# Attention scores of a gated recurrence: the matmuls and copies of each head cut to the blocks that the masks keep, in pieces of 32 queries

## What is computed

```python
G = jnp.cumsum(gc, axis=-2)                       # log decays, summed within a chunk of 64
diff = G[:, :, :, None, :] - G[:, :, None, :, :]
decay = jnp.exp(jnp.where(mask, diff, -jnp.inf))  # mask: key s <= query t
att = jnp.einsum('bhtk,bhsk,bhtsk->bhts', qc, kc, decay)
o = o_inter + jnp.einsum('bhts,bhsv->bhtv', att, vc)
```

## Time and profile before

| | |
|---|---|
| median of 3 executions | 2349.55 us (2348.75 to 2355.37) |
| profiled execution, first to last instruction | 2347.9 us |
| PE busy | 2281.0 us, 97% |
| DVE busy | 1565.2 us, 67% |
| ACT busy | 1268.0 us, 54% |
| POOL busy | 1337.0 us, 57% |
| score matmuls (L1168), 816 records | 30.3 us busy |
| large score copies (L2671), 48 | 35.1 us busy |
| small score copies (L2678), 24 | 5.3 us busy |

### The profile page before, as it was taken

How to read it: one execution, slowest core, us unless ns; L and a number is a source line. 1 busy time by engine, 2 the same in 40 slices (tenths; PEclk the granted TensorE clock), 3 DMA queues, 4 the chain that set the end, 5 groups by cost and what they waited for, 6 DMA issues and landing times.

```text
span 2347.9 us, 54490 instructions
## 1 busy us (share of the span) xinstructions
PE 2281.0 (97%) x20432; PEld 1959.8 (83%) x20432; DVE 1565.2 (67%) x2618; ACT 1268.0 (54%) x2295; POOL 1337.0 (57%) x1019
## 2 busy tenths in 40 slices
PE   8899999999998999999999999999999999999998
PEld 6788888888887888888878888877888888888886
DVE  7877777635589777777882332389687767445755
ACT  6454555433576666666554334554555544334775
POOL 2787777767515555555555444305777778677120
PEclk9999999999999999999999999999999999999999
DMA  3123222443530111111111212330232222535202
GB/s 132 50 83 101 92 77 86 151 143 103 166 100 20 40 46 46 44 39 41 49 43 49 63 48 86 115 101 28 86 92 89 86 77 86 178 122 194 76 19 75
DMA packets 155236, 194.93 MB, mean 83 GB/s; under 512 B 13168, under 2 KB 102512, under 8 KB 155120
## 3 DMA queue, kind: packets, MB, share of 16 engines
q1 hardware_dynamic: 111920, 153.59, 20.7%
q10 hardware_dynamic: 43200, 39.83, 5.2%
HBM read 155.49 MB, written 37.88 MB: 82 GB/s over the span
## 4 chain that ended last, share of the span: by engine, by line
PE 65%; DVE 13%; POOL 7%; issue 6%; ACT 5%; DMA 3%; SPq 1%; ACTq 0%; POOLq 0%; DVEq 0%
PE bank L1068 17%; PE bank L1071 17%; PE bank L1070 17%; PE bank L1035 4%; PE bank L1037 4%; PE bank L1036 4%; POOL ring L929 4%; DMA ring<-weights 3%; POOL ring L933 2%; DVE hid L2201 2%; DVE hid L2355 1%; DVE ops L2256 1%; DVE ops L2365 1%; DVE ops L2209 1%; PE bank L1201 1%
## 5 line engine op out<-in xcount | busy, mean ns | idle before, releaser
L1068 PE MATMUL bank<-ops,ring 128*128 128x264 f16 x4112 | 1139.4, 277 | 20.2 <-DVE work L2402 6.3
L1070 PE MATMUL bank<-ops,ring 128*128 128x264 f16 x4112 | 1138.7, 277 | 0.0
L1071 PE MATMUL bank<-ops,ring 128*128 128x264 f16 x4112 | 1138.6, 277 | 0.0
L929 POOL TENSOR_TENSOR ring<-ring 128x512 f16<-128x512 f32 (+1 forms) x492 | 659.8, 1360 | 273.8 <-ACT ring L1401 273.8
L1401 ACT ACTIVATE ring<-ring 128x512 f16<-128x512 f32 (+1 forms) x492 | 286.7, 614 | 501.8 <-POOL ring L933 498.3
L1068 PEld LDWEIGHTS bank<-ops,ring 128*128 128x128 f16 x4112 | 404.4, 98 | 91.3 <-issue 9.8
L1071 PEld LDWEIGHTS bank<-ops,ring 128*128 128x128 f16 x4112 | 403.7, 98 | 61.7
L1070 PEld LDWEIGHTS bank<-ops,ring 128*128 128x128 f16 x4112 | 403.7, 98 | 60.3
L914 POOL TENSOR_TENSOR ring<-wtmp,ring 128x512 f16<-128x512 f32 x107 | 130.8, 1227 | 340.9 <-ACT ring L1342 340.3
L1035 PE MATMUL bank<-hid,ring 128*128 128x264 f16 x1068 | 294.9, 276 | 1.5 <-issue 1.3
L1037 PE MATMUL bank<-hid,ring 128*128 128x264 f16 x1068 | 294.8, 276 | 0.0
(11 more groups left out here) (227 smaller groups left out, 3626.5 us busy)
## 6 DMA issues: line engine op xcount, KB each, us to landing
ring<-weights SPq DMA_DIRECT2D x363, 256.0 KB, 2.7
ops<-spill SPq DMA_DIRECT2D x16, 1056.0 KB, 6.9
ring<-weights SPq DMA_DIRECT2D x120, 128.0 KB, 2.4
spill<-hid ACTq DMA_DIRECT2D x42, 264.0 KB, 2.9
spill<-hid ACTq DMA_DIRECT2D x20, 528.0 KB, 5.0
ops<-spill SPq DMA_DIRECT2D x8, 792.0 KB, 5.1
hid<-xT SPq DMA_DIRECT2D x8, 528.0 KB, 8.3
hid<-out_x ACTq DMA_DIRECT2D x8, 528.0 KB, 7.3
```

The lines of the kernel that those rows point to most:

```text
L929: nc.gpsimd.tensor_tensor(low(slot, kh), weight_source(name, k, kh), high(slot, kh), ALU.subtract)\
L1068: nc.tensor.matmul(out, whi, xhi, start=(kk == 0 and fresh(name, k)), stop=False, skip_group_check=True)
L1070: nc.tensor.matmul(out, whi, xlo, start=False, stop=False, skip_group_check=True)
L1071: mm = nc.tensor.matmul(out, wlo, xhi, start=False, stop=end, skip_group_check=True)
```

## The change

`head_scores` computes only the pieces that a mask can keep, always 32 query columns wide, and all 17 chunks now lie 32 columns apart in the bank.
- L32: the chunk's keys 0 to 31 by its queries 32 to 63. 17 matmuls, each 32 x 32.
- L16: all 64 keys by the 32 queries that are in the last 16 of a block of 32 (two runs of 16 columns). 17 matmuls, each 64 x 32.
- D16: the two diagonal blocks of 32, as two matmuls of 32 x 32. 34 matmuls, whose results lie in partitions 0, 32, 64 and 96 onwards.

`evac_scores` follows. L32's kept part is a full rectangle, so it is a plain `tensor_copy`, 2 of 32 x 256 and 1 of 32 x 32. L16 takes 4 predicated copies of 64 x 128 and 2 of 64 x 16, D16 takes 4 of 32 x 256 and 2 of 32 x 32. The masks, the banks, the waits and the places in all queues are as before.

```diff
+            def score_parts(kind, kk, qq, c):
+                k0 = c * C
+                if kind == "L32":
+                    return [(0, kk[:, k0:k0 + 32], qq[:, k0 + 32:k0 + C])]
+                if kind == "L16":
+                    return [(0, kk[:, k0:k0 + C], qq[:, k0:k0 + C].rearrange("p (b t) -> p b t", b=2)[:, :, 16:32])]
+                return [(32 * n, kk[:, k0 + 32 * n:k0 + 32 * n + 32], qq[:, k0 + 32 * n:k0 + 32 * n + 32]) for n in range(2)]
...
-                            h0 = C * (c % 2)
-                            last = nc.tensor.matmul(bank[b][h0:h0 + C, (c - c0) // 2 * C:((c - c0) // 2 + 1) * C],
-                                                    kk[:, c * C:(c + 1) * C], qq[:, c * C:(c + 1) * C],
-                                                    start=True, stop=True)
+                            at = (c - c0) // 2 * 32
+                            for row, keys, queries in score_parts(kind, kk, qq, c):
+                                h0 = C * (c % 2) + row
+                                out = bank[b][h0:h0 + keys.shape[1], at:at + 32]
+                                if kind == "L16":
+                                    out = out.rearrange("p (b t) -> p b t", b=2)
+                                last = nc.tensor.matmul(out, keys, queries, start=True, stop=True)
...
-                    for h0 in (0, C):
-                        ins = V_.copy_predicated(att[h0:h0 + C, 0:PT // 2 * P].rearrange(
-                            "p (j s c) -> p j s c", s=2, c=C)[:, :, h0 // C, :],
-                            msk[h0:h0 + C, m, :].rearrange("p (j c) -> p j c", c=C),
-                            b[h0:h0 + C, 0:512].rearrange("p (j c) -> p j c", c=C))
+                    if kind == "L32":
+                        for h0 in (0, C):
+                            ins = V_.tensor_copy(att_pairs(h0, h0 + 32)[:, :, h0 + 32:h0 + C],
+                                                 b[h0:h0 + 32, 0:256].rearrange("p (j t) -> p j t", t=32))
+                    elif kind == "L16":
+                        for h0 in (0, C):
+                            for n in range(2):
+                                t0 = 32 * n + 16
+                                ins = V_.copy_predicated(
+                                    att_pairs(h0, h0 + C)[:, :, h0 + t0:h0 + t0 + 16],
+                                    msk[h0:h0 + C, 1, :].rearrange("p (j t) -> p j t", t=C)[:, :, t0:t0 + 16],
+                                    b[h0:h0 + C, 0:256].rearrange("p (j n t) -> p j n t", n=2, t=16)[:, :, n, :])
+                    else:
+                        for p0 in range(0, P, 32):
+                            t0 = p0 % C
+                            ins = V_.copy_predicated(
+                                att_pairs(p0, p0 + 32)[:, :, p0:p0 + 32],
+                                msk[p0:p0 + 32, 2, :].rearrange("p (j t) -> p j t", t=C)[:, :, t0:t0 + 32],
+                                b[p0:p0 + 32, 0:256].rearrange("p (j t) -> p j t", t=32))
...
```

More of the change, by code:

```diff
@@ L2666, in evac_tok, with att_pairs, evac_scores, own @@
                     evac(head, kind, r, lambda b: copy(b, j0, j1))
-            def evac_scores(head, kind, m):
+            def att_pairs(p0, p1):
+                return att[p0:p1, 0:PT // 2 * P].rearrange("p (j t) -> p j t", t=P)
+            def evac_scores(head, kind):
+                tail = PT // 2 * P
                 def pairs(b):
-                    for h0 in (0, C):
-                        ins = V_.copy_predicated(att[h0:h0 + C, 0:PT // 2 * P].rearrange(
-                            "p (j s c) -> p j s c", s=2, c=C)[:, :, h0 // C, :],
-                            msk[h0:h0 + C, m, :].rearrange("p (j c) -> p j c", c=C),
-                            b[h0:h0 + C, 0:512].rearrange("p (j c) -> p j c", c=C))
+                    if kind == "L32":
[17 more added lines that the diff above has]
+                                b[p0:p0 + 32, 0:256].rearrange("p (j t) -> p j t", t=32))
+                    return ins
+                def own(b):
+                    if kind == "L32":
+                        return V_.tensor_copy(att[0:32, tail + 32:tail + C], b[0:32, 0:32])
+                    for n in range(2):
+                        if kind == "L16":
+                            t0 = 32 * n + 16
+                            ins = V_.copy_predicated(att[0:C, tail + t0:tail + t0 + 16], msk[0:C, 1, t0:t0 + 16],
+                                                     b[0:C, 16 * n:16 * n + 16])
+                        else:
+                            p0 = 32 * n
+                            ins = V_.copy_predicated(att[p0:p0 + 32, tail + p0:tail + p0 + 32],
+                                                     msk[p0:p0 + 32, 2, p0:p0 + 32], b[p0:p0 + 32, 0:32])
@@ L2675, in pairs @@
                     return ins
                 evac(head, kind, 0, pairs)
-                evac(head, kind, 1, lambda b: V_.copy_predicated(att[0:C, PT // 2 * P:TP], msk[0:C, m, 0:C],
-                                                                 b[0:C, 0:C]))
+                evac(head, kind, 1, own)
             def chunks(a, w):
@@ L2779, in head_turn @@
                 sums_b_odd("heads", p0, b0)
-                evac_scores(hh, "L32", 0)
+                evac_scores(hh, "L32")
                 operand(W[4], K_, hh, 6)
@@ L2784, in head_turn @@
                     onorm_low(h - 2, W[5])
-                evac_scores(hh, "L16", 1)
+                evac_scores(hh, "L16")
                 sums_b_even("heads", p0, b0)
-                evac_scores(hh, "D16", 2)
+                evac_scores(hh, "D16")
                 operand(W[5], Q, hh, 9)
```

## The result

The changed kernel takes 2361.95 us (median of 6 executions, 2357.79 to 2366.78). Beside it the kernel before took 2349.62 us (6 executions, 2346.22 to 2355.37). The ratio is 1.0044, with an interval of [1.0031, 1.0057]. The prediction was 2347.5 us in a range of 2342.5 to 2352.0, with a chance of 0.07 for slower: wrong in sign and size. The profiled execution of the changed kernel spans 2358.1 us, against 2347.9 before.

What follows compares the result with a forecast made beforehand. The prediction took each turn as bound by 23.7 us of weight preparation, then 31.7 us of PE. 8 x 0.2 us plus 0.4 in head 8 gave 2.0 us off, so 2347.5 us, range 2342.5 to 2352.0.

Steps and rivals of the forecast that it cites:

- PE's change: Score clusters on PE: L32 saves 0.45 us, L16 nothing, D16 0.3; 0.75 us less per head.
- The cover: First part of a turn: PE's saving only lengthens its standstill, from 0.44 to about 1.2 us; worth 0 on the path.
- the same picture in all eight turns: Heads' stage: every turn is 23.7 us of weight preparation, then 31.7 us of PE.
- DVE's change: Score evacuations on DVE: L32 saves 0.69 us, L16 saves 0.17, D16 costs 0.44; net 0.42 us per head saved.
- The later steps follow: Weight chain after POOL's low parts: third sum, last low parts, DMA, scaling and copy all keep POOL's 0.2 us lead.
- Worth 0.2 us a head: Weight chain through POOL: DVE's earlier start brings POOL out 0.2 us earlier per head, bounds 0 and 0.4.
- POOL loses in the turns: Rival: POOL's first sum falls behind a multiply, 0.8 us later, costing 8 x 0.8 us; 2355.6 us, chance 0.04.
- The turns at the first sum: After L32's evacuation: DVE's multiplies and POOL's sums alternate; multiply to 868.2, sum to 869.3, multiply to 870.4, sum to 871.5.
- No new dips: PE's clock in the heads: standstills of 1.2 us should not bring it below 1.00.

Runs made afterwards that it cites:

- early: Changed kernel with the two multiplies that make the D16 operands moved ahead of sums_b_odd and L32's evacuation; 2342.88 us, ratio 0.996.
- only_d16: Kernel before with only the D16 part of the change, L32 and L16 as before; 2354.85 us, ratio 1.0017.
- shift_before: Kernel before with 17 small 32 by 32 matmuls added on PE ahead of the loop over the heads; 2354.65 us, ratio 1.0012.
- the three realigned kernels: 47 small matmuls ahead of the heads' loop, added to the changed kernel (1.0037), with two multiplies moved ahead (0.9944), or with its last multiply delayed by two copies (1.0).
- only_l32: Kernel before with only the L32 part of the change, matmuls and copies, L16 and D16 as before; 2360.25 us, ratio 1.0032.

## Why the prediction was wrong

- **PE's change: right.** L32's body 0.56 us (0.59 predicted), L16 as before, D16 0.60 us, at the best end of its range (0.75 taken). The Trainium skill's page TensorEngine Tiling (Array Packing), section Instruction Overhead, speaks of some 60 cycles for each matmul and advises against cutting a dimension that is already small. At 2.4 GHz the 60 cycles of the Trainium skill are 25 ns (an estimate from its figure). That is below the 58 ns of before, so it did not say that L32 would save nothing, as the prediction read it. Within one strip the 32-column records start some 33 ns apart, which does not contradict the figure. But the strips do not queue for it: L32's 34 records start 17 ns apart on average and D16's 68 records 9 ns. The advice does not fit here: cut to 32 by 32, L32's body takes 0.56 us instead of 1.04, and D16's, with twice the matmuls, 0.60.
- **The cover: right.** PE saved 0.9 us a turn and stood still for it. (Of "the same picture in all eight turns" the waits of before show six, 1.7 us together.) early proves the cover from the other side: without the hole, the same saving is worth 0.98 us a turn.
- **DVE's change: right** to 5 ns in each group of copies.
- **"The later steps follow": this step failed.** The prediction played the turns of DVE and POOL through from 866.9 to 874.95 and stopped there, since POOL came out 0.2 us early. Its own numbers, carried on for DVE, would have shown the collision. The second multiply was to end at 870.4. From the end of the two multiplies (867.59 + 4.29 = 871.88) to 876.25 DVE needed 4.37 us before, and L16 and D16 together add 0.27, so the last multiply would start at 875.0. POOL's third sum was due at 875.10 - 0.2 = 874.9. What had been 1.15 us apart was to be 0.1 apart, with 1.1 us a turn at stake on who comes first. "Worth 0.2 us a head" was in truth between 0.2 gained and 1.1 lost. The sum had 8 x 0.2 = 1.6 us gained for it; the seven turns lost 5.6. That this sum comes so near to the measured place (875.0 - 864.16 = 10.9 us of the turn, 10.95 measured) is luck: the two multiplies ended 1 us sooner than played through, and DVE then waited 0.95 us for PE. The rival that named the loss ("POOL loses in the turns", 0.04) had the mechanism at the wrong instruction: the first sum, where the loss (2.1 us and more) does close again.
- **The turns at the first sum: mis-sized.** Both multiplies ran back to back (2.47 us) with POOL waiting behind them (3.33), not one by one. It made no difference for POOL's later times, but it set DVE free 1 us earlier (5.2 us of the turn instead of 6.2), and so up to its wait for PE.
- **No new dips: wrong.** The argument was made for holes of 0.44 and 1.2 us. The holes became 2.2 to 2.3 from start to start, and one of five brought a dip of 1.7 us. Nor was 1.2 us safe: in only_d16 PE stood still for 1.13 us in head 8, from 1155.4 us on, and its clock read 0.50 from 1157.7 on.
- **Not thought of: code length.** 17 more matmuls moved the moments at which PE's code is fetched, 1000 us behind the change: +3.7 us in the profiled execution. That the length does it is shown by shift_before and the three realigned kernels. That it acts through the packet amid the weight tiles is read from where the packet lies in fourteen traces; no run moved the packet by anything but the length.

In sum: +1.5 ahead of the heads, 7 turns +5.6 (1.7 of it the dip), -0.6 from head 8 to the second down projection, and +3.7 in that. What stays open is why one code packet delays tiles by up to 2 us when it lasts about 1 us. It is also open why POOL's first sum of the heads comes 0.7 us earlier to 4.8 us later than before from kernel to kernel, without relation to the edits. So up to 1.5 of the 10.2 us need not be the change's.

## What to carry to other kernels

When an engine off the critical path gets faster, list each place where it shares something with an engine on the path, and work out for each who comes first, before and after. Carry that to the end of the turn: a margin below the error of the forecast is a coin toss at the price of a whole instruction. And before cutting work that stands under a cover, move the collision out of the way first; here two moved multiplies made the same cut worth 0.98 us a turn. If a change lengthens one engine's unrolled code, look at the transfer-bound stages behind it, too.

## What the runs showed of the hardware that was not expected

- DVE's multiplies and POOL's sums, both full width in SBUF, hold each other up by whole instructions. That was read before; what was not expected is how little decides it. A lead of 0.04 to 0.08 us settles which of the two takes 1.3 us and which 2.35. At 0.02 us the starts no longer tell: in the second turn of only_l32 POOL's record starts first and takes 2.43 us all the same. DVE's copies out of PSUM beside POOL's three low parts cost them nothing (3.40 us for three).
- A second DVE multiply right behind the first kept its place: POOL's sum waited for both (3.33 us), though in the kernel before, where POOL's first sum had started first, the two engines alternated (4.29 us for the two multiplies).
- fp32 matmuls of 32 weight columns on four column strips: 68 records start within 0.60 us, about as long as 34 on two strips take (0.56 us).
- Code fetches are traffic: one packet of 16,384 bytes of instructions, about 1 us long, beside loads of weights. Their phase, moved by 4352 bytes, went with 2.7 to 5.9 us more in a stage of 240 us (up to 7.6 with dips of the clock).
